# A mixer block with sixteen routed experts: the second expert's first product in plain float32, and the expert weights w1 and w3 loaded in another layout

## The reference, cut to what matters

```python
def moe_ffn(h, router_w, router_b, w1, w3, w2):
    scores = jax.nn.sigmoid(jnp.dot(h.astype(F32), router_w.astype(F32)))
    ...
    gates = jnp.sum(jax.nn.one_hot(idx, N_EXPERTS, dtype=F32) * wsel[..., None], axis=1)
    y = jnp.zeros(h.shape, F32)
    for e in range(N_EXPERTS):
        he = jax.nn.silu(h @ w1[e]) * (h @ w3[e])
        y = y + gates[:, e:e + 1] * (he @ w2[e]).astype(F32)
    return y.astype(h.dtype)
```

## Time and profile before

| | |
|---|---|
| median of 3 runs | 586.81 us (586.78 to 587.27) |
| the profiled execution | 587.05 us, its span 585.2 us |
| PE busy | 549.8 us, 94% |
| DVE busy | 450.1 us, 77% |
| ACT busy | 325.1 us, 56% |
| DMA | 171.81 MB, mean 294 GB/s |
| granted TensorE clock, mean | 0.985 |

### The profile page before, as it was taken

The page is one execution under the profiler, slowest core; times in us unless marked ns, Lnnn a source line. Parts: engine busy times, 40 slices in busy tenths (PEclk is TensorE's granted clock), DMA queues, the critical chain, the costliest instruction groups (busy, mean ns, idle before and its releaser), DMA issues.

```text
span 585.2 us, 7667 instructions
## 1 busy us (share of the span) xinstructions
PE 549.8 (94%) x2733; PEld 417.7 (71%) x2733; DVE 450.1 (77%) x592; ACT 325.1 (56%) x405; POOL 155.4 (27%) x141
## 2 busy tenths in 40 slices
PE   1789999999998999989999899999999999999995
PEld 1345875677676787857687788888888888877772
DVE  1348699446586546477999899999999999989867
ACT  4541133535435922266586496677886676966624
POOL 5000833223310700020781321233311333200070
PEclk9799999999999999999999899999999999999998
DMA  8999994878224720149979999999999999999665
GB/s 295 390 372 318 378 379 178 275 207 316 73 72 157 239 73 37 60 160 390 342 282 392 393 324 393 393 392 393 392 387 391 390 393 390 361 375 361 201 217 214
DMA packets 88746, 171.81 MB, mean 294 GB/s; under 512 B 5379, under 2 KB 18887, under 8 KB 88721
## 3 DMA queue, kind: packets, MB, share of 16 engines
q1 hardware_dynamic: 82578, 153.34, 73.4%
q10 hardware_dynamic: 2768, 9.97, 4.2%
q0 software_dynamic: 3376, 8.18, 3.9%
HBM read 158.06 MB, written 17.32 MB: 300 GB/s over the span
## 4 chain that ended last, share of the span: by engine, by line
PE 80%; DMA 6%; DVE 6%; ACT 3%; issue 3%; SPq 1%; DVEq 0%; ACTq 0%
PE psum L896 6%; PE psum L1244 4%; PE psum L1246 4%; PE psum L1245 4%; PE psum L1271 4%; PE psum L1273 4%; PE psum L1272 4%; PE psum L1256 4%; PE psum L1255 4%; PE psum L1254 4%; PE psum L904 4%; DMA w<-in_moe_w 3%; PE psum L941 3%; DMA ada<-in_ada_w 3%; PE psum L943 3%; PE psum L942 3%
## 5 line engine op out<-in xcount | busy, mean ns | idle before, releaser
L2245 DVE TENSOR_TENSOR w_lo<-w,w_hi 128x2048 fp32r<-128x2048 f32 x32 | 72.9, 2282 | 1.2 <-ACT w_hi L1669 1.2
L2234 DVE TENSOR_TENSOR w_lo<-w,w_hi 128x1024 fp32r<-128x1024 f32 (+2 forms) x30 | 68.6, 2292 | 0.0
L1660 ACT CAST w_hi<-w 128x2048 fp32r<-128x2048 f32 x30 | 57.3, 1911 | 16.3 <-PE psum L1256 13.7
L1669 ACT CAST w_hi<-w 128x2048 fp32r<-128x2048 f32 x32 | 60.4, 1918 | 7.3 <-DVE ysb L2267 6.1
L2228 DVE TENSOR_TENSOR w_lo<-w,w_hi_a 128x2048 fp32r<-128x2048 f32 (+1 forms) x30 | 51.6, 1757 | 3.9 <-ACT w_hi_a L1648 3.4
L1271 PE MATMUL psum<-w_hi,heT_hi 128*128 128x512 f32 x120 | 49.8, 415 | 0.8 <-DVE w_lo L2245 0.8
L1851 DVE SCALAR_TENSOR_TENSOR rows<-ada,cc,rows 128x512 f32<-128x512 f32 x48 | 41.8, 874 | 8.9 <-DMA ada<-in_ada_w 7.4
L762 POOL COPY idx<-idx 128x1 int32 x12 | 9.9, 826 | 141.5 <-PE psum L1217 141.5
L1273 PE MATMUL psum<-w_hi,heT_lo 128*128 128x512 f32 x120 | 47.2, 394 | 0.0
L1272 PE MATMUL psum<-w_lo,heT_hi 128*128 128x512 f32 x120 | 47.1, 393 | 0.0
L1245 PE MATMUL psum<-w_lo,xgT_hi 128*128 128x512 f32 x120 | 46.8, 390 | 0.0
(11 more groups left out here) (368 smaller groups left out, 1271.6 us busy)
## 6 DMA issues: line engine op xcount, KB each, us to landing
w<-in_moe_w SPq DMA_DIRECT2D x32, 2048.0 KB, 13.5
w<-in_moe_w SPq DMA_DIRECT2D x32, 1024.0 KB, 13.8
ada<-in_ada_w SPq DMA_DIRECT2D x12, 2048.0 KB, 18.2
win<-in_w_in SPq DMA_DIRECT2D x8, 1024.0 KB, 14.5
expert_rows<-ysb ACTq DMA_DIRECT2D x15, 512.0 KB, 6.3
expert_rows<-zero SPq DMA_DIRECT2D x1, 5120.0 KB, 21.1
wout<-in_w_out SPq DMA_DIRECT2D x4, 1024.0 KB, 4.9
x<-in_x SPq DMA_DIRECT2D x2, 1024.0 KB, 10.0
```

The source lines that it names most:

```text
L1669: act.copy(w2_hi[:, :, hs], w2_sb[b][:, :, hs]).then_inc(w2_hi_ok[half], 1)
L2234: v.tensor_tensor(w3_lo[b][:, ks, :], w3_sb[b][:, ks, :], w3_hi[:, ks, :], ALU.subtract).then_inc(w3_lo_ok, n)
L2245: v.tensor_tensor(w2_lo[b][:, :, hs], w2_sb[b][:, :, hs], w2_hi[:, :, hs], ALU.subtract).then_inc(w2_lo_ok[half], 1)
```

## The change

Five things, in the order of the diff:

- A new tile `xgT_1` holds the turned rows of block 1 unsplit.
- w1 and w3 of every expert but the first are loaded so that partition p gets rows 8p to 8p + 7: one piece of 16 KB. `rows_in` takes the matching channels: tile k is every eighth channel from k on, so that the operand of the transpose is read with a step of 8 elements, 32 bytes.
- SP asks for `w3[1]` only when the gather of block 1 has landed (`xg_in[1]`).
- The w1 product of block 1 is 8 plain float32 matmuls on `xgT_1` (`plain1_second`) instead of 24 float32r ones. ACT's four casts and DVE's three subtractions for that w1 are gone; ACT has one more copy, of the turned rows. `hidden3` of that block still uses the split rows.
- On ACT and DVE the steps around it are put in another order.

```diff
-                sp.dma_start(sb[e][:], which[0, e].rearrange("(k p) f -> p k f", p=P)).then_inc(sem_[e], 16)
+                order = "(k p) f -> p k f" if e == 0 else "(p k) f -> p k f"
+                sp.dma_start(sb[e][:], which[0, e].rearrange(order, p=P)).then_inc(sem_[e], 16)
...
             load_first_w2(0)
+            sp.wait_ge(xg_in[1], 16)
             load_first(moe_w3, w3_sb, 1, w3_in)
...
-                sp.dma_start(w1_sb[b][:], moe_w1[0, bass.ds(e, 1)].rearrange("a (k p) f -> p (a k) f", p=P)
+                sp.dma_start(w1_sb[b][:], moe_w1[0, bass.ds(e, 1)].rearrange("a (p k) f -> p (a k) f", p=P)
...
+                every = xg[b].rearrange("t (p k) -> t k p", k=KD)
                 for k in range(KD):
-                    m = pe.transpose(bank[k // 4][:, (k % 4) * P:(k % 4 + 1) * P], xg[b][:, k * P:(k + 1) * P], ident[:])
+                    m = pe.transpose(bank[k // 4][:, (k % 4) * P:(k % 4 + 1) * P], every[:, k, :], ident[:])
...
+            def plain1_second():
+                pe.wait_ge(w1_in[1], 16)
+                pe.wait_ge(x0_ok, KD + 1)
+                pe.wait_ge(sg_ok, 1)
+                for k in range(KD):
+                    if k == 4:
+                        hidden_turned(0)
+                    m = pe.matmul(bank[2][:], xgT_1[:, k, :], w1_sb[1][:, k, :], start=(k == 0), stop=(k == KD - 1))
+                m.then_inc(h1_ok, 1)
...
-            hidden1(1, 1, 0)
+            plain1_second()
             expert_out0(0, 0)
+            pe.wait_ge(x_lo_ok, 2)
             hidden3(1, 1)
...
+            act.wait_ge(xt_ok, 2)
+            act.copy(xgT_1[:].rearrange("p k t -> p (k t)"), psum[:, 0:2, :].rearrange("p a n -> p (a n)")
+                     ).then_inc(x0_ok, 1)
             high_rows(1)
             act.wait_ge(w3_in[1], 16)
             high_w3(1, 0)
+            high_w3(1, 1)
             high_hidden(0, 0)
-            high_w3(1, 1)
+            act.wait_ge(w1_in[0], 32)
+            for g in range(4):
+                high_w1_part(0, g)
             gate_half(1)
-            high_w1(0, 2, 1)
```

More of the change, by code:

```diff
@@ L167, in build @@
         ysb = [at(f"ysb_{b}", (176 + 4 * b) * K1, [P, D]) for b in range(2)]
+        xgT_1 = at("xgT_1", 180 * K1, [P, KD, P])
         xgT_0 = at("xgT_0", 160 * K1, [P, KD, P])
@@ L591, in load_w3 @@
                 sp.wait_ge(h3_ok, s - 1)
-                sp.dma_start(w3_sb[b][:], moe_w3[0, bass.ds(e, 1)].rearrange("a (k p) f -> p (a k) f", p=P)
+                sp.dma_start(w3_sb[b][:], moe_w3[0, bass.ds(e, 1)].rearrange("a (p k) f -> p (a k) f", p=P)
                              ).then_inc(w3_in[b], 16)
@@ L1712, in _ @@
                     store_h2(3)
[L1713 to L1716, removed]
                 act.wait_ge(x0_ps, k + 1)
@@ L1721, in _ @@
             act.sem_inc(xt_ok, 1)
-            high_w1_part(1, 2)
-            high_w1_part(1, 3)
+            act.sem_inc(w1_hi_ok, 4)
             high_w2(0, 0, 0, 0)
@@ L2298, in overflow_list @@
                 v.tensor_copy(ints[:, 0:9], ovf[:, 0:9]).then_inc(route_ok, 1)
-            low_w1(1, 1, 0, 2)
+            v.sem_inc(w1_lo_ok, 4)
             overflow_blocks()
-            low_w1(1, 1, 2)
-            low_w1(1, 1, 3)
+            low_w2(0, 0, 0)
+            low_w2(0, 0, 1)
             low_rows(1)
-            low_w2(0, 0, 0)
             gated(0)
@@ L2309, in _ @@
             overflow_list()
+            low_w3(1, 1, 0, 2)
             low_hidden(0, 0)
-            low_w3(1, 1, 0, 2)
             low_w3(1, 1, 2, 2)
-            low_w2(0, 0, 1)
+            low_w1(0, 2, 0, 2)
             v.wait_ge(rows_act, 8)
             expert_rows(0, 0, 0, 0)
-            low_w1(0, 2, 0, 2)
             gated(1)
```

## The result

| | before | after |
|---|---|---|
| median of six runs | 586.79 us (586.35 to 587.76) | 593.92 us (590.68 to 595.73) |
| profiled execution | 587.05 us, span 585.2 | 595.73 us, span 593.5 |
| ratio of the times | | 1.0116 (95% interval 1.0089 to 1.0143) |

The change makes the kernel 1.2% slower. The forecast was 587.4 us in a range that ended at 592.0, so the time lies outside it. Lines of `kernel.py` stand 2 to 15 further down after the change: the turning of `he` is L1278 (L1264 before), the store of the expert rows L1696 (L1681).

What follows compares the result with a forecast made beforehand. The experts were taken as bound by PE's own work. 587.05 + 1.25 + 0 + 0 - 1.18 + 0.5 = 587.62 us, less 0.24 for the median, gave 587.4; range 585.4 to 592.0.

Steps and rivals of the forecast that it cites:

- Term 1: Block 1's w1 product on PE: plain matmuls take 6.95 us against 5.70 for the split ones, +1.25 us.
- Term 2: Work saved on DVE and ACT: 0 us; DVE idles ahead of block 1's `he`, block 2's 2.54 us wait stays.
- Term 3: Order around block 1, `w3[1]` asked for after the gather: 0, up to +1.3 us; gather 1 to 3 us sooner.
- Term 4: 16 KB runs for w1 and w3: about 429 GB/s, no late load by block 13, -1.18 us.
- Term 5: Transposes read with a 32-byte step, 120 on PE's path: 0 to +1.0 us, taken as +0.5.
- Rival 2: Strided load of the transposes sets PE's pace: 94 ns x 120 = 11.3 us on the path, 598.7 us; chance 0.13.
- The rivals: Relief reaches block 2's wait (0.10); strided load slows PE (0.13); 16 KB runs no faster (0.12); w3[1] late (0.07).

Runs made afterwards that it cites:

- the kernel with the later split: Changed kernel with three more ACT instructions, DVE's split of expert 0's second w2 half moved back behind expert 1's w3 split; 586.48 us, ratio 0.9999 to before.

## Why the prediction was wrong

The step that failed is the 0 for the new order in terms 2 and 3: the prediction asked what DVE and ACT save and when `w3[1]` arrives, and put at nothing, without a reason, what the moved and missing instructions do to ACT's code and to POOL. The runs showed two costs in its place: 4.2 to 5.0 us for ACT's late code and 2.4 to 2.6 us for POOL held up beside DVE's two w2 splits, with what the clock adds behind it.

**Term 1, the plain product, was right.** In the kernel with the later split, where PE's clock stays at 1.00, it takes 6.99 us with the turning inside (288.84 to 295.83) against 6.06 before, +0.93, and the stretch from there to block 1's turning is 9.94 instead of 9.53. Together +1.34, forecast +1.25. The 0.41 us stand at the first float32r matmul behind the product, whose successor starts 0.63 us after it instead of 0.23. Without the turning (292.36 to 292.80) the product takes 6.55 us up to that matmul, and with these 0.40 us the 6.95 of block 0's product. Kernel against kernel (16 KB runs and wait, with and without the plain product) the ratios are 0.9999 and 0.9990, 0.5 us, with intervals that overlap.

**Term 2 was right on the wait it looked at and missed the bill.** DVE stood idle for 4.62 us (4 to 6 forecast), and with ACT's code wait taken away block 2's stall is 2.58 us (2.2 to 2.8 forecast). But I looked only at what DVE and ACT save, and not at what else moves when instructions are taken out and moved up. Two things did:

- Three ACT instructions fewer: the 5.23 us issue. With them back, block 2's turning comes 20.53 us after block 1's and block 3's 17.85 after that (24.05 and 20.57 in the table). In medians it is 5.0 us (593.92 and 588.93), by the ratios 0.72%, 4.2 us. No row of the trace before could have given its size, but the code packet at 307.5, 3.1 us ahead of the store, was there to be seen.
- The two w2 splits moved up beside `hot_mod`: PE's index product starts 16.04 us after block 0's w1 product instead of 14.74, +1.30, and in this trace the clock behind the wait makes the plain product 1.7 us longer (8.68 against 6.99); in the trace with 2 KB runs it doesn't. In medians 2.4 us (588.93 and 586.48), by the ratios 2.6. I had `hot_mod` in the trace and didn't ask what would run beside it.

With 0.41 (the start, which is no effect of the change), 1.30, 1.34 and 1.69 and a rest of 0.15 the 4.89 us by which block 1's turning is late in this pair of traces are accounted for.

**Term 3, the order: not what costs, and it protects.** The gather of block 1 landed 3.6 us after its issue instead of 5.8, and `w3[1]` was there at 289.09, both as forecast. ACT waited 2.21 us for it, and PE for none of it. The wait alone costs 0.25%. I had priced the wait as a delay of the load behind it, and hadn't given the earlier gather a price; with 16 KB runs it is the gather that counts, 4.4 us between the medians of 590.11 and 585.69.

**Term 4, -1.18: right in size.** Blocks 13 and 14 are 1.21 us shorter, ACT waits for no load there, and full stretches move 416 to 434 GB/s (429 estimated). The median landing of a 2 MB load fell from 13.5 to 9.4 us. No trace with 16 KB runs has the stall, and four of the five with 2 KB runs have one. The fifth, the kernel before with three instructions fewer, has blocks 13 and 14 in 17.84 and 17.88 us with 2 KB runs, so other things can take the stall away too.

**Term 5, taken as +0.5: measured 0.** The loads of the turned rows grew as the nearest row had them:

```profile
L1221 PEld LDWEIGHTS psum<-ident,xg x104: 185/191/230, 335.4 to 552.0; 128*128 128x128 f32 x104
```

191 ns instead of 141, but seven steady blocks (370.81 to 495.86) take 17.86 us each, against 17.88. The load stays hidden. Of the rule on lines of 16 bytes in the Trainium skill ("SBUF — State Buffer", the section on the DMA port swizzle), a load of 50 ns more is what can be seen; PE's pace shows nothing of it. Rival 2 with its 11.3 us is refuted.

**The rivals.** None of the four was the one that came. The range was built from the priced edits alone, and its slower end from their sum; what a change does to the place of other instructions in the code, and to what runs beside them, had no case of its own.

## What to carry to other kernels

An edit that adds or removes instructions on an engine can also shift where that engine waits for its code; here it did, at ACT's first DMA issue in its loop, in both directions. If a DMA issue or another cheap instruction shows a duration of microseconds with "issue" as the reason behind it, look for a packet of an instruction queue just then, and move the position by a few harmless instructions before judging the edit itself. When work moves up on DVE, ask what GpSimd does at that time and who waits for it; and before making DMA pieces larger, find the small transfer that an engine waits for and that will stand between them, and order it ahead.

## What the runs showed that I had not expected

- The same unchanged stretch, 38 to 50 us, has a granted clock of 0.86 in some profiled executions and 1.00 in others, as in the row above. That could cost up to 1.7 us (0.14 of 12 us, an estimate), but no run shows that it does: block 0's w1 product starts at 271.35 us in the trace before, with 1.00, and at 270.82 in one with 0.86.
- The dip behind block 2's stall of about 2.5 us came in only some kernels: block 3 took 19.2 to 19.5 us before, with the wait alone, and with 16 KB runs and wait; it took 17.8 to 18.0 with 16 KB runs alone, 4 KB runs, and the kernels with the plain product and three instructions more. The former had 1.00 at 38 to 50 us, the latter 0.86. Whether the one decides over the other is open, and so is the larger spread of single runs (583.8 to 588.6 us for the kernel before) that it may explain.
- The change without SyncE's wait has a median of 597.94 us, but its profiled execution took 593.34, the lowest of five. What cost the other four runs 4 us isn't in the trace; a gather that landed as late as with 16 KB runs alone would fit, and isn't shown.
